# First rows turned by a diagonal of their inverse root, with bias-line products behind the turns

## The reference, cut to what matters

```python
def rms_norm(x, g, eps=1e-6):
    y = xf * lax.rsqrt(jnp.mean(xf * xf, axis=-1, keepdims=True) + eps)
    return (y * g.astype(jnp.float32)).astype(x.dtype)
...
    hn = rms_norm(h, attn_norm[l])          # h: 16 meta rows and 256 rows of x
    proj = hn @ w_in[l]                     # w_in: 1024 x 1952
    ...                                     # three kinds of attention, feed-forward, second block
        bias = bias_tab[t5_bucket(q_pos[:, None], k_pos[None, :])]
```

## Time and profile before

| | us |
|---|---|
| median of 3 runs | 961.72 |
| lowest and highest of them | 958.26, 963.18 |
| the profiled execution | 960.17 |
| its span | 958.4 |
| TensorE busy in the span | 917.6 |
| VectorE busy | 629.6 |
| ScalarE busy | 464.7 |

### The profile page before, as it was taken

The page is one execution under the profiler, slowest core; times in us unless marked ns, Lnnn a source line. Parts: engine busy times, 40 slices in busy tenths (PEclk is TensorE's granted clock), DMA queues, the critical chain, the costliest instruction groups (busy, mean ns, idle before and its releaser), DMA issues. The chain is left out here.

```text
span 958.4 us, 17499 instructions
## 1 busy us (share of the span) xinstructions
PE 917.6 (96%) x6858; PEld 819.3 (85%) x6858; DVE 629.6 (66%) x1339; ACT 464.7 (48%) x924; POOL 156.5 (16%) x111
## 2 busy tenths in 40 slices
PE   4999989999999999989999999999999999999998
PEld 1987678999999989879988898998888889999996
DVE  4567666665557587797997977545956665445543
ACT  5553564554445455374334674354454464454451
POOL 2000000000000007000975315000000023233221
PEclk9999999999999999999999999999999999999999
DMA  8540233475565544546542202022555546555551
GB/s 304 174 138 23 88 111 132 133 233 163 177 220 164 188 161 158 176 131 221 172 136 68 67 5 76 2 70 89 168 184 184 189 152 215 184 176 176 190 184 44
DMA packets 38678, 139.61 MB, mean 146 GB/s; under 512 B 4330, under 2 KB 4586, under 8 KB 38596
## 3 DMA queue, kind: packets, MB, share of 16 engines
q1 hardware_dynamic: 37184, 134.17, 42.6%
q10 hardware_dynamic: 884, 2.49, 0.8%
q0 software_dynamic: 528, 1.84, 0.6%
HBM read 137.39 MB, written 1.08 MB: 144 GB/s over the span
## 5 line engine op out<-in xcount | busy, mean ns | idle before, releaser
L1804 DVE TENSOR_TENSOR parts<-raw,parts 128x1024 fp32r<-128x1024 f32 (+2 forms) x225 | 286.7, 1310 | 143.0 <-ACT parts L1297 139.2
L1297 ACT ACTIVATE parts<-raw 128x1024 fp32r<-128x1024 f32 (+2 forms) x225 | 228.3, 1049 | 125.1 <-PE psum L531 95.9
L529 PE MATMUL psum<-hT,parts 128*128 128x256 f32 (+1 forms) x928 | 265.4, 286 | 3.4 <-DVE hT L1821 2.0
L530 PE MATMUL psum<-hT,parts 128*128 128x256 f32 (+1 forms) x928 | 264.0, 284 | 0.0
L531 PE MATMUL psum<-hT,parts 128*128 128x256 f32 (+1 forms) x928 | 262.3, 283 | 0.0
L529 PEld LDWEIGHTS psum<-hT,parts 128*128 128x128 f32 x928 | 176.3, 190 | 6.9 <-DVE hT L1821 2.9
L531 PEld LDWEIGHTS psum<-hT,parts 128*128 128x128 f32 x928 | 177.5, 191 | 0.0
L530 PEld LDWEIGHTS psum<-hT,parts 128*128 128x128 f32 x928 | 176.7, 190 | 0.6
L529 PE MATMUL psum<-parts,arena_r 128*128 128x512 f32 x344 | 135.1, 393 | 3.7 <-issue 3.0
L531 PE MATMUL psum<-parts,arena_r 128*128 128x512 f32 x344 | 134.0, 389 | 0.0
L530 PE MATMUL psum<-parts,arena_r 128*128 128x512 f32 x344 | 133.9, 389 | 0.0
(11 more groups left out here) (324 smaller groups left out, 1183.7 us busy)
## 6 DMA issues: line engine op xcount, KB each, us to landing
raw<-weights SPq DMA_DIRECT2D x247, 512.0 KB, 4.2
raw<-weights SPq DMA_DIRECT2D x4, 384.0 KB, 7.1
X<-x SPq DMA_DIRECT2D x2, 512.0 KB, 6.2
out<-X SPq DMA_DIRECT2D x2, 512.0 KB, 2.6
arena<-lines POOLq DMA_DIRECT2D x1, 768.0 KB, 9.5
cbuf<-consts ACTq DMA_DIRECT2D x1, 561.0 KB, 5.2
arena<-lines POOLq DMA_DIRECT2D x1, 544.0 KB, 7.3
arena<-params ACTq DMA_DIRECT2D x1, 512.0 KB, 8.7
```

The source lines that it names most:

```text
L529: mm(ps, a, c, start=start, stop=False)
L530: mm(ps, a, d, start=False, stop=False)
L1297: signal(A(split_slot(name)[0], whole_piece, ACT.Copy), "first_parts")
L1804: signal(V_.tensor_tensor(second, whole_piece, first.bitcast(F32), ALU.subtract), "split_vector")
```

## The change

The rows are no longer scaled before they are turned. VectorE makes three small diagonal matrices, identity times the inverse root of each row (turner_meta, 16x16, and turners, two of 128x128), and TensorE multiplies the raw rows with them, which scales and turns at once. These are ordinary fp32 matmuls in place of transposes. The two line products stand behind the turns, on TensorE and on ScalarE. While the turns' and lines' jobs are closed, `limit` is set so that ScalarE and VectorE split nothing beyond cq0. ScalarE issues three loads in the opening (cbuf, pbuf, one-hot); held and final are issued behind the store of the lines. VectorE waits for held after its last part of the turned rows. The scratch of the lambda sums moves to other columns, and functions that no longer serve are removed.

```diff
+        turner_meta = scr[0:META, TT * P:TT * P + META]
...
-            pe.wait_ge(sem("const_in"), 64)
+            taken[0] = 1
+            limit[0] = "in1_cq0"
+            pe.wait_ge(sem("norm1"), 3)
+            for k in range(KD):
+                ps = opened(f"h1_{k}")
+                cols = slice(P * k, P * k + P)
+                mm(ps[:, 0:META], one["Xm"][0:META, cols], turner_meta, start=True, stop=True)
+                for t in range(TT):
+                    last = mm(ps[:, META + P * t:META + P * t + P], X[:, t, cols], turners[:, t, :], start=True, stop=True)
+                closed(last, f"h1_{k}")
+                arrivals[k] = f"h1_{k}"
+            pe.wait_ge(sem("onehot_in"), 16)
             pe.wait_ge(sem("relneg"), 1)
             for v in range(2):
                 ps = opened(f"line{v}")
...
-            taken[0] = 1
-            pe.wait_ge(sem("norm1"), 2)
-            pe.wait_ge(sem("norm1_act"), 1)
-            Xn = one["Xn"].rearrange("p (t n) -> p t n", t=TT)
-            transposes_of(Xn, lambda k: f"h1_{k}", meta=one["Xnm"])
+            limit[0] = None
...
             act.dma_start(cbuf[:, :], consts[:, 0:NCHELD]).then_inc(sem("const_in"), 16)
-            act.dma_start(att1["held"], consts[:, NCHELD:NEARLY]).then_inc(sem("const_in"), 16)
-            act.dma_start(att1["S"][:, 0:NLATE - NEARLY], consts[:, NEARLY:NLATE]).then_inc(sem("const_in"), 16)
             act.dma_start(pbuf[:, :], params[:, 0:NHELD]).then_inc(sem("const_in"), 16)
-            act.dma_start(att1["final"], params[:, NHELD:NPARAM]).then_inc(sem("final_in"), 16)
+            act.dma_start(att1["S"][:, 0:NLATE - NEARLY], consts[:, NEARLY:NLATE]).then_inc(sem("onehot_in"), 16)
...
-            second_tile("1", jn)
+            turned_out(lambda k: f"h1_{k}", hT, ALL, lambda k: par("attn_norm")[:, k:k + 1])
             act.wait_ge(sem("meta_zero"), 2)
...
             act.dma_start(line_dram, att1["PTm"][0:BH, 0:2 * LINE]).then_inc(sem("lines_out"), 16)
-            turned_out(lambda k: f"h1_{k}", hT, ALL, lambda k: par("attn_norm")[:, k:k + 1])
+            act.dma_start(att1["held"], consts[:, NCHELD:NEARLY]).then_inc(sem("held_in"), 16)
+            act.dma_start(att1["final"], params[:, NHELD:NPARAM]).then_inc(sem("final_in"), 16)
...
+            dve.wait_ge(sem("const_in"), 32)
+            a = PARAM["rel"][0]
+            signal(V_.memset(pbuf[32:33, a:a + BH], NEG), "relneg")
             dve.wait_ge(sem("sq1"), 3)
             inv_rms(st[:, 4:7], st[:, 0:3], D, st[:, 24:27], st[:, 27:30], "rms1")
-            dve.wait_ge(sem("const_in"), 64)
-            a = PARAM["rel"][0]
-            signal(V_.memset(pbuf[32:33, a:a + BH], NEG), "relneg")
-            Xn = one["Xn"].rearrange("p (t n) -> p t n", t=TT)
-            signal(V_.tensor_scalar(Xn[:, 0, :], X[:, 0, :], st[:, 4:5], None, ALU.mult), "norm1")
-            signal(V_.tensor_scalar(one["Xnm"][0:META, :], one["Xm"][0:META, :], st[0:META, 6:7], None, ALU.mult), "norm1")
+            signal(V_.tensor_scalar(turner_meta, ident[0:META, 0:META], st[0:META, 6:7], None, ALU.mult), "norm1")
+            for t in range(TT):
+                signal(V_.tensor_scalar(turners[:, t, :], ident, st[:, 4 + t:5 + t], None, ALU.mult), "norm1")
...
             turned_rest(lambda k: f"h1_{k}", hT, ALL, lambda k: par("attn_norm")[:, k:k + 1])
+            dve.wait_ge(sem("held_in"), 16)
             dve.wait_ge(sem("lamexp"), 1)
```

More of the change, by code:

```diff
@@ L538, in need, with transposes_of @@
                     freed(pe, arrivals.pop(k))
-            def transposes_of(src, name_of, meta=None, turn_of=lambda k: ident, ks=range(KD)):
+            def transposes_of(src, name_of, ks=range(KD)):
                 for k in ks:
@@ L544, in transposes_of @@
                     ps = opened(name)
[L545 to L548, removed]
                     for t in range(TT):
-                        last = nc.tensor.transpose(ps[:, at + P * t:at + P * t + P], src[:, t, P * k:P * k + P], turn_of(k))
+                        last = nc.tensor.transpose(ps[:, P * t:P * t + P], src[:, t, P * k:P * k + P], ident)
                     closed(last, name)
@@ L828, in _ @@
             out1_part(2, 1, lambda: first_rows(0))
[L830 to L833, removed]
             tok = slice(0, SEQ)
@@ L1326, in half_sums @@
                         signal(square_sums(X[:, t, s_], 2 * nh + t, junk[:, t, s_]), tag)
-            def second_tile(which, dst):
-                act.wait_ge(sem("rms" + which), 1)
-                signal(A(dst[:, 1, :], X[:, 1, :], ACT.Copy, scale=st[:, 5:6]), "norm" + which + "_act")
             def exponentials(g):
@@ L1951, in _ @@
             signal(V_.memset(st[:, 2:3], 1.0), "meta_column")
+            dve.wait_ge(sem("const_in"), 32)
+            a = PARAM["rel"][0]
+            signal(V_.memset(pbuf[32:33, a:a + BH], NEG), "relneg")
             dve.wait_ge(sem("sq1"), 3)
             inv_rms(st[:, 4:7], st[:, 0:3], D, st[:, 24:27], st[:, 27:30], "rms1")
-            dve.wait_ge(sem("const_in"), 64)
-            a = PARAM["rel"][0]
-            signal(V_.memset(pbuf[32:33, a:a + BH], NEG), "relneg")
-            Xn = one["Xn"].rearrange("p (t n) -> p t n", t=TT)
-            signal(V_.tensor_scalar(Xn[:, 0, :], X[:, 0, :], st[:, 4:5], None, ALU.mult), "norm1")
-            signal(V_.tensor_scalar(one["Xnm"][0:META, :], one["Xm"][0:META, :], st[0:META, 6:7], None, ALU.mult), "norm1")
+            signal(V_.tensor_scalar(turner_meta, ident[0:META, 0:META], st[0:META, 6:7], None, ALU.mult), "norm1")
+            for t in range(TT):
+                signal(V_.tensor_scalar(turners[:, t, :], ident, st[:, 4 + t:5 + t], None, ALU.mult), "norm1")
             lam = par("lam").rearrange("p (r n) -> p r n", r=4)
             for n in range(2):
-                ins = V_.tensor_tensor_reduce(out=scr[:, 32 * n:32 * n + DQK], in0=lam[:, 2 * n, :], in1=lam[:, 2 * n + 1, :],
+                ins = V_.tensor_tensor_reduce(out=scr[:, 384 + 32 * n:384 + 32 * n + DQK], in0=lam[:, 2 * n, :], in1=lam[:, 2 * n + 1, :],
                                               scale=1.0, scalar=0.0, op0=ALU.mult, op1=ALU.add,
```

## The result

The changed kernel takes 969.79 us (median of 6 runs, 969.25 to 972.29), the kernel before 960.04 in the runs beside it: a ratio of 1.0101 (95% interval 1.0086 to 1.0116), 9.75 us slower. The forecast was 964 and its range ended at 969. The profiled execution took 969.25, its span is 967.4, against 960.17 and 958.4 before.

The account below looks back on a forecast made before the run. TensorE, busy 917.6 of 958.4 us, was taken as the bound, so the opening's timing decides: -2.8 + 3.65 + 2.0 = +2.9 us on 960.17 gives 963.1, plus 1.55 for the median 964.6, said as 964; range 958 to 969.

Parts of the forecast that it names:

- Bound, scaling: Opening: what the first pieces' products gain comes back whole; with small scalings turns start at 13.8, 2.2 us earlier.
- Turns: Turning rows on TensorE: a product costs two transposes; a k takes 1.35 us at the low clock, 0.70 at the higher.
- The bound of 10.8 us for eight: Turns on TensorE: the upper bound for all eight k, at the low clock's 1.35 us each; the lower was 5.6.
- Clock during turns: New turns count as products: 5.1 us of low clock, then the higher one; turns end at 21.85.
- low through the turns: Rival: the clock stays low through the turns, cq1 starts at 34.2, +5.1 us, 965.5 to 967; chance 0.12.
- Lines: Line products behind the turns on TensorE: four records at half of 0.665 us, 1.4 us; cq0 starts at 23.3.
- Split and wait for held: Ahead of cq1: VectorE waits for held, landing 3.25 us after issue; cq1 starts at 29.95 after a 3.65 us pause.
- Clock after the pause: Behind the pause ahead of cq1: products run at the low clock again, costing 1.2 to 3.4 us, taken as 2.0.
- Covered: Later pieces, bias rows and final add nothing; dk1's load is needed over 14 us after cq1 starts, so hidden.
- The sum: Whole kernel: -2.8 (TensorE ready earlier) + 3.65 (pause) + 2.0 (clock) = +2.9 us.
- The 1.55 us that I added for the median of three runs: The runs' median lies 1.55 us above the profiled execution, which takes the forecast from 963.1 to 964.6.

Follow-up runs that it names:

- warmed: The kernel before with ten fp32 products of ones, never read, on TensorE while it waits in the opening: 959.7 us, ratio 0.9992.
- the changed kernel warmed: The changed kernel with ten fp32 products of ones ahead of the turns: 963.93 us, ratio 1.005 to the kernel before.
- warmed and without 16-row products: The changed kernel with the 16-row products left out of the turns and ten products of ones ahead: 960.01 us, ratio 0.9997.
- the third warmed kernel: The changed kernel with ten products of ones ahead, held loaded in the opening and no limit on splitting: 960.33 us, ratio 0.9994.

## Why the prediction was wrong

By its own steps:

*Bound, scaling:* right in the main: 7.7 of the 9.1 us stand at the start of cq1. Turns started at 13.59 (13.8 said).

*Turns:* "4 x 0.213 + 0.41 + 0.09 = 1.35" was 1.69 at the low clock. The terms: 1.15 for the four big records and 0.54 for the two small ones. The row with the 16-row products left out gives 0.91 for four (of 544 columns in all), which is the 0.213 for 128 columns that I used. In the mixed turns only the two middle records keep to it; those beside a 16-row product start 0.35 to 0.37 apart from the next (read in the run with dense matrices). So it is the mixing that costs; that exposed weight loads are the reason is my guess. The bound of 10.8 us for eight was no bound: they took 13.5. At the high clock 0.96, not 0.70. That a product costs two transposes back to back was right: 32 records, two a product, from 15.30 to 18.90 at the high level, 0.11 each. The Trainium skill (TensorE: Matmul & The Clock Gate, Terms) has a factor of four for fp32, and the trace bears out two.

*Clock during turns:* this is the step that failed. "So I let the new turns count as products and take 5.1 us of low clock." The row it rested on, fp32 products at 94 us, has wide products with no 16-row ones between. Its own rival, low through the turns, had 0.12. The low clock and the dearer k move turns, lines and cq0: turns ended at 27.08 for 21.85, cq0 started at 29.84 for 23.3, and TensorE was ready for cq1 at 35.2 for 26.3. Of these 8.9 us 2.5 are the k time (turns at 1.35 and the low level throughout would have ended at 24.6) and the other 6.4 the low clock: 2.7 in the turns, 1.4 in the lines, 2.3 in cq0. The page's sentence on transposes, in the Trainium skill (TensorE: Matmul & The Clock Gate, Part 4: PE-mode transpose), agrees with the trace again: warmed, the clock fell during the transposes of the kernel before, at 17.3. But it fell in the ordinary products with the diagonals too, at 15.3, so these runs don't single out transposes. What I drew from the page, that turns by ordinary products must do better, doesn't follow.

*Lines:* 2.8 us, since the clock was low, not 1.4.

*Split and wait for held:* the mechanism was right, held landed in 3.6 (3.25 said) and VectorE waited 6.43 for it. But cq0 was late and slow itself and covered most of it: the pause was 1.55, not 3.65. *Clock after the pause:* it didn't fall there in the changed kernel, behind 1.55 us. It did behind 2.38 (the changed kernel warmed) and 3.71 (warmed and without 16-row products). The length of the pause does not decide it by itself, though: ahead of the values it fell behind 1.06 in two runs, and behind 1.95 it fell with the dense matrices and held in the changed kernel.

*Covered:* wrong for dk1. I asked when TensorE needs it. ScalarE and VectorE split it in their order, ahead of the latent sums, and ScalarE stood 4.17 us for its load. 1.7 us came in behind cq1 in the changed kernel (0.4 of it the idle time on VectorE, for which no load shows as the reason), 2.7 in the one with transposes (1.89 late at cq1, 4.56 at 55 us), where the clock fell behind the pause of 2.22.

The sum against the measured terms: turns, lines and cq0 -2.8 said, +6.1 measured (35.2 for 29.1); pause 3.65 and 1.55; what came later 2.0 (as a low clock) and 1.4. 2.9 said, 9.0 in the spans. I forecast slower and was 6 us short: 8.9 in the clock and the k time of the turns, of which 2.7 were given back by a smaller pause and less behind it. The 1.55 us that I added for the median of three runs did not come back: the six runs beside the changed kernel have their median at 960.04.

**What stays open.** What VectorE waits for in the 0.5 us that lengthen the pause ahead of the values. Why 16-row products among the others keep the clock low. Whether transposes with their 16-row ones grouped ahead would raise and hold the clock as the grouped products did: no run tried it, so nothing here says that the diagonal is the better way to turn. And how much of each median is where the clock falls later: behind 45 us the profiled executions have 10.2 to 20.5 us at the low level, in stretches of 3.4 or 6.8 us at different places (near 50, 94, 126 and 430), worth up to 5 us by half their length. The executions of one kernel differ in the same way: with one piece ahead 958.38 us at a mean granted clock of 0.994 and 962.73 at 0.989. That 2 us won at cq1 showed as 0 to 1 in several medians fits this, but it wasn't tested.

## What to carry to other kernels

Before putting the start of a stage on a rising clock, look for stretches of the same mix of instructions, not just of the same type: narrow products between wide ones cost more than their columns, and here they left the clock low. When a piece of work is moved later, follow every engine that handles it in order, not only the one that needs the result. And idle TensorE time at the start is free for products that raise the clock, but what follows decides what they are worth: here the clock fell in the mixed turns of each profiled execution and held in the grouped ones.

## What the runs showed of the hardware that I had not expected

- Fp32 turns with a 16-row product between the 128-row ones: 1.69 us a k at the low level, against 0.91 with the same 272 columns in two products. At the high level 0.96 and 0.47. With the 16-row products grouped ahead 0.21 us a record of either kind at the low level and 0.11 at the high.
- 13.5 us of such turns with TensorE busy all the time left the clock low. Products of 128 columns back to back, behind the grouped 16-row ones, were followed by its rise 4.2 us after their start, at 21.0. Dense or diagonal made no difference.
- After products of ones had raised it, the clock fell 1.9 us (at 15.3) and 2.8 us (at 16.3) after the mixed diagonal turns began in two runs, and 1.4 us after the mixed transposes began (at 17.3). Not in every execution of one kernel: mean granted clocks from 0.982 to 0.993 in nine executions of the third warmed kernel, 965.74 to 956.78 us.
- Products of ones, which are never read, raise the clock as others do: it rose at 4.4 us, 3 us after the first of them, and was high through all turns, 0.11 us a record.
- Behind pauses of TensorE the clock fell after 1.06, 1.57, 1.95, 2.38 and 3.71 us in some traces and held after 1.05, 1.55 and 1.95 in others.
